# A mixture-of-experts kernel: the order in which an expert's tokens are laid over its 64 slots

## The reference, cut to what matters

```python
def hierarchical_moe(h, wg_router, bg_router, we_router, be_router, w_gate, w_up, w_down):
    g_sel = jnp.argmax(g_logits, axis=-1)
    ...
    top_v, top_i = lax.top_k(e_in, TOP_K_EXPERTS)
    ...
    for g in range(N_GROUPS):
        a = jnp.einsum('nd,edf->nef', hf, w_gate[g])
        b = jnp.einsum('nd,edf->nef', hf, w_up[g])
        hid = jax.nn.silu(a) * b * gates[:, g, :, None].astype(hf.dtype)
        out = out + jnp.einsum('nef,efd->nd', hid, w_down[g])
```

## Time and profile before

| what | value |
|---|---|
| runs of the kernel before | 1487.17, 1493.5, 1494.14 us; median 1493.5 us |
| profiled execution: span, first to last instruction | 1483.8 us |
| profiled execution: its own time | not given beside the span; the fastest run shown is 3.4 us above the span, the median 9.7 us |
| PE busy over the span | 1401.5 us (94%) |
| DVE, ACT, POOL busy | 888.6, 427.9, 57.3 us |
| granted PE clock, mean | 0.989 |
| bytes moved by DMA | 202.00 MB |

### The profile page before, as it was taken

One profiled execution on the slowest core, in us unless ns is written; L12 is line 12 of the kernel. 1 busy time (PEld: TensorE's weight loads), 2 busy tenths in 40 slices (PEclk: granted clock), 3 DMA queues, 4 the chain that ended last, 5 costly groups with the idle time before them and its releaser, 6 DMA issues. The chain is left out here.

```text
span 1483.8 us, 15654 instructions
## 1 busy us (share of the span) xinstructions
PE 1401.5 (94%) x5612; PEld 833.3 (56%) x5612; DVE 888.6 (60%) x1951; ACT 427.9 (29%) x706; POOL 57.3 (4%) x114
## 2 busy tenths in 40 slices
PE   7999999999999989999999999998899798999886
PEld 3455555657567758888887444445485445333222
DVE  5567688898897947767476449965473424222111
ACT  2434444454445315101112233134413430000000
POOL 0000000000000000000000000000000001122211
PEclk9999999999999999999999999999999999999999
DMA  7031010122110124232233121001123658999995
GB/s 293 29 114 57 29 57 29 58 72 65 49 58 29 43 107 164 85 109 90 95 137 109 49 83 60 15 15 78 63 80 127 272 197 322 402 407 405 409 411 174
DMA packets 38972, 202.00 MB, mean 136 GB/s; under 512 B 6896, under 2 KB 8816, under 8 KB 32112
## 3 DMA queue, kind: packets, MB, share of 16 engines
q1 hardware_dynamic: 31600, 186.29, 33.2%
q0 software_dynamic: 4608, 8.40, 2.3%
q10 hardware_dynamic: 2688, 6.29, 1.1%
HBM read 196.77 MB, written 12.58 MB: 141 GB/s over the span
## 5 line engine op out<-in xcount | busy, mean ns | idle before, releaser
L565 PE MATMUL gla_proj<-hT,weight_slots 128*128 128x512 f32 x672 | 295.1, 592 | 1.9 <-DVE hT L1035 1.9
L565 PEld LDWEIGHTS gla_proj<-hT,weight_slots 128*128 128x128 f32 x672 | 125.1, 190 | 147.7 <-issue 146.9
L3328 PE MATMUL moe_banks<-weight_slots,moe_room 128*64 128x512 f32 x400 | 95.2, 626 | 14.9 <-DMA weight_slots<-in_w_gu 12.3
L2062 PE MATMUL mid_p_proj<-hT,weight_slots 128*128 128x512 f32 x208 | 93.0, 594 | 1.8 <-PEq L187 1.8
L3485 DVE SCALAR_TENSOR_TENSOR moe_room<-moe_banks,moe_kept,moe_room 128x256 f32<-128x256 f32 x16 | 7.7, 484 | 131.1 <-ACT moe_room L3440 131.1
L734 ACT ACTIVATE gla_level_decay<-gla_level_decay 128x1024 f32<-128x1024 f32 x56 | 59.1, 1055 | 49.5 <-DVE gla_level_decay L922 49.1
L3328 PEld LDWEIGHTS moe_banks<-weight_slots,moe_room 128*64 128x64 f32 x400 | 29.7, 143 | 71.8 <-issue 56.4
L2062 PEld LDWEIGHTS mid_p_proj<-hT,weight_slots 128*128 128x128 f32 x208 | 39.1, 190 | 52.1 <-issue 52.1
L692 ACT COPY gla_raw<-gla_proj 128x512 f32<-128x512 f32 x38 | 22.4, 589 | 137.5 <-PE gla_proj L565 137.5
L593 PEld LDWEIGHTS gla_level<-gla_level_q,gla_level_k 128*128 128x128 f32 x448 | 55.0, 192 | 8.4 <-issue 6.7
L593 PE MATMUL gla_level<-gla_level_q,gla_level_k 128*128 128x128 f32 x448 | 56.4, 275 | 0.9 <-DVE gla_level_k L933 0.9
(11 more groups left out here) (529 smaller groups left out, 2658.4 us busy)
## 6 DMA issues: line engine op xcount, KB each, us to landing
weight_slots<-in_w_gu SPq DMA_DIRECT2D x25, 2048.0 KB, 22.7
weight_slots<-in_w_gla SPq DMA_DIRECT2D x40, 512.0 KB, 3.6
weight_slots<-in_w_dn SPq DMA_DIRECT2D x10, 2048.0 KB, 28.8
weight_slots<-in_w_merge SPq DMA_DIRECT2D x32, 512.0 KB, 4.8
weight_slots<-in_w_out SPq DMA_DIRECT2D x16, 512.0 KB, 4.4
weight_slots<-in_w_v SPq DMA_DIRECT2D x3, 2048.0 KB, 7.4
hT<-in_w_gu SPq DMA_DIRECT2D x3, 2048.0 KB, 36.6
weight_slots<-in_w_u SPq DMA_DIRECT2D x8, 512.0 KB, 4.4
```

What stands on the lines that cost most here:

```text
L565: last = nc.tensor.matmul(pj[:, n % 2, :], lhsT, rhs, start=(k == 0), stop=(k == KT - 1))
L2062: last = nc.tensor.matmul(pw[:, n % 2, :], a, b, start=(k == 0), stop=(k == KT - 1))
L3328: last = nc.tensor.matmul(pG[rows, e, :], hgT[:, k, rows], core.as_gate_up(at[k // 4])[:, x, k % 4, :], start=(k == 0), stop=(k == KT - 1))
```

## The change

A new constant `slot_rank` holds, for each of the 64 slots, the rank of the token that sits in it. It is loaded into 64 new columns of `moe_kept` (`rank_of`). Both comparisons that make `at_slot` use it in place of 0 to 63. The first 64 ranks go, in order, to the slots

```diff
-        kept = ctx.enter_context(nc.sbuf_tensor("moe_kept", [P, 2 * NB + CAP + 8 * NB + NB + 2 * (P + 4) + 4 + 8], F32))
+        kept = ctx.enter_context(nc.sbuf_tensor("moe_kept", [P, 2 * NB + 2 * CAP + 8 * NB + NB + 2 * (P + 4) + 4 + 8], F32))
...
+        self.rank_of = take(CAP)
...
         sp.dma_start(iota, dram["moe_iota"][:, 0:CAP]).then_inc(aux, 16)
+        sp.dma_start(lot.rank_of, dram["slot_rank"][:]).then_inc(aux, 16)
         core.load_part(sp, 6)
...
-        pe.wait_ge(aux, 80)
+        pe.wait_ge(aux, 96)
...
-        dve.wait_ge(aux, 80)
+        dve.wait_ge(aux, 96)
...
-        chain(equal(at_slot, CAP, slot))
+        chain(nc.vector.tensor_tensor(at_slot, lot.rank_of.unsqueeze(1).to_broadcast([P, 2 * NB, CAP]),
+                                      slot.unsqueeze(2).to_broadcast([P, 2 * NB, CAP]), ALU.is_equal))
...
+    rank = np.arange(CAP)
+    turn, pick = (rank // 8) % 2, rank % 8
+    place = 8 * pick + 4 * ((pick // 4) ^ turn) + rank // 16
+    slot_rank = np.zeros(CAP, np.float32)
+    slot_rank[place] = rank
+    extra["slot_rank"] = np.ascontiguousarray(np.broadcast_to(slot_rank, (P, CAP)))
```

More of the change, by code:

```diff
@@ L3530, in list_rounds @@
                 chain(equal(at_unit[:, :, (n - 1) * EXPERTS:n * EXPERTS], EXPERTS, lot.unit_off))
-            chain(equal(at_slot, CAP, lot.slot))
+            chain(nc.vector.tensor_tensor(at_slot, lot.rank_of.unsqueeze(1).to_broadcast([P, 2 * NB, CAP]),
+                                          lot.slot.unsqueeze(2).to_broadcast([P, 2 * NB, CAP]), ALU.is_equal))
             nc.vector.tensor_tensor(slot_id, at_slot, lot.ids.unsqueeze(2).to_broadcast([P, 2 * NB, CAP]), ALU.mult)
```

## The result

Six runs of the changed kernel give a median of 1480.22 us (1477.86 to 1481.35), six of the one before 1490.93 us (1486.85 to 1494.14; three of them are those shown ahead of the prediction, with the higher median of 1493.5). The ratio is 0.9935, 95% interval 0.9919 to 0.9951: 9.7 us faster at 1490.93 us (7.3 to 12.1), against 8.0 forecast. The whole time lies 5.3 us under the 1485.5 us forecast: 2.6 us because I took 1493.5 for the kernel before, 2.7 because the medians are 10.7 us apart and not 8.0.

A forecast was written before the change was run, and what follows sets the result against it. DMA engines were taken to bound the expert loop, the fullest setting its end. Gains of 6.6 + 1.1 + 0.3 = 8.0 us, taken from the 1493.5 us median, gave 1485.5 us, range 1478 to 1491.

The forecast's parts named there:

- What bounds it: Expert loop: DMA engines bound it; they drop out one after another after 1440 us, the fullest setting the end.
- Rule B: Rows to engines by 8 * (partition >> 6) + ((partition >> 2) & 7): fullest engine goes from 93 rows to 71.
- A: Row-to-engine rule giving the fullest engine 64 rows over the mean, up to 34 us; the prediction excluded it.
- Rule C: Row-to-engine rule making the new order the uneven one, 128 rows against 78: slower, 1520 us, chance 0.02.
- Part 45 lands sooner: Load for the second half of pair 15's gate and up: lands at 1453.7 instead of 1460.27, gain 6.6 us.
- the factor 0.75: Loop's end: the fullest engine's measured excess over the counted one, 10.4 to 13.9 us, used to scale row costs.
- 16.1 us of unchanged work: From pair 15's second gate and up half (1460.27) to the last scatter (1476.39): no slack, stays the same.
- The last scatter: End of the kernel: fullest engine goes from 8 rows to 5, gain 1.1 us, bound 1.5.
- The first gather: Start of the loop, PE waits its 4.1 us in full: fullest engine from 8 rows to 6, gain 0.3 us.
- the perfectly even case: Rival for the loop's end: the 7 rows left over weigh nothing, gain 10.9 us, 1482.6 us, chance 0.12.
- Late issue: Rival: engines drop out because the last parts were issued late; only 1.4 us gained, 1492.1 us, chance 0.17.
- Slow engines: Rival: the last engine is slow by nature, not full; engines 7 and 15 get more rows, 1507 us, chance 0.04.

The follow-up runs named there:

- uneven by B: The change with another rank table, 121 rows on the fullest engine and 8 on the emptiest by Rule B: 1501.64 us, ratio to before 1.0089.
- mirrored: The change's table replaced by the old order read backwards (rank 0 in slot 63), engines 7 and 15 fullest: 1488.26 us, ratio to before 1.0001.
- even by B: The change with another rank table, 75 rows on the fullest engine and 50 on the emptiest by Rule B: 1479.13 us, ratio to before 0.9936.
- rotated: The change with each eight ranks starting three engines further on, 69 rows on the fullest engine instead of 71: 1476.76 us, ratio to before 0.9912.

## Why the prediction was right, point by point

- **What bounds it.** Right. The area under the shares gave an even finish at 1462.4, 224.0 us after the first gather. The changed kernel's area from 1440 to 1470 is 5 x 5.22 = 26.1 us, at 1.01 gone by 1465.8, 223.5 us after its first gather. The mean engine has the same work to the same time; only the last one moved.
- **Rule B.** Right. Two tables that split A from B, 22 us apart in their medians, and six that lie within 2 us of one line of B's counts show it. Rule C falls with the change itself, which is as uneven by C as can be (128 and 0) and got faster. The Trainium skill's formula (DMA: Bandwidth & Descriptors, the section on the descriptor swizzle) names the engines for a transfer of 128 partitions; what the runs add is that it holds, as far as counts can show, for an indirect DMA with part of its rows skipped: a skipped row leaves its engine nearly free and moves nobody else's. Nearly, since it still counts as a packet: with every row skipped, POOL's queue had 3744 packets in 1260 to 1430 and took 1.2% of the 16 engines' time, some 9 ns a packet.
- **Part 45 lands sooner (6.6 us, and 0.3 through the first gather).** Right in kind, 1.4 us too small. PE's last half started 8.3 us sooner after the first gather. The term that was mis-sized is the 7 rows left over, for which I took 2.7 us by the factor 0.75. The PE row at 1467.29 waits for part 47 until then, 225.0 us after the first gather; taken with the even finish of 224.0 or 223.5 that leaves 1.0 to 1.5 us. The spacing behind it was right: 11.5 us from the wait for part 45 to that for part 47, 11.4 forecast.
- **16.1 us of unchanged work.** Nearly. In the old timeline the down matmuls of pair 14 started at 1467.78 after 0.77 us marked as issue; in the changed one they follow at once, and the stretch takes 15.3 us in every even order. I had taken all of it for work, but these 0.8 us were a wait for weights, for part 46. Its load was issued at 1410.50 before and at 1406.60 with the change, and the DMA rows of these issues (the last number is us from issue to landing) are, before and changed:

```profile
weight_slots<-in_w_dn SPq DMA_DIRECT2D x1, 2048.0 KB, 57.2
```

```profile
weight_slots<-in_w_dn SPq DMA_DIRECT2D x1, 2048.0 KB, 55.4
```

So part 46 landed at 1467.7 before, just as the matmuls started, and at 1462.0 with the change, half a us before they did.
- **The last scatter (1.1 us).** From its issue to the end of the span 7.4 us before, 6.7 and 7.0 with the change, 7.5 with the order uneven by B and 7.9 mirrored. From issue to landing it took 5.8 us before, 5.8 uneven by B and 6.3 mirrored, against 5.1 and 5.4 with the change, 4.9 even by B and 5.3 rotated: the two groups don't overlap, and their means are 0.8 us apart. The sign is right and the size about two thirds; "under 5 us" came true in one of the four even profiles only.
- **The first gather (0.3 us).** 4.14 us before, 3.98 and 3.93 now, 3.86 and 3.90 in the other even orders. The gather gained 0.2 us, but PE's turn behind it took 1.98 us instead of 1.53, in the uneven orders too, so nothing of it was left behind the turn.
- **The comparison and the new load.** Nothing, as forecast: the 128x512 comparison takes 0.70 us in the chain as before, and the load stands at 1190.55 to 1190.98, before anything waits. From the stage's first load to the first gather it is 56.5 us in both profiles.

Of the rivals, the perfectly even case was closer to the 9.9 us than the forecast was: its 10.9 us (10.7 with the 1.1 us that the forecast has for the last scatter; its own sum says 1.3) is 1.0 too much, the 8.0 are 1.9 too little. The rows that were left over weighed little, 1.0 to 1.5 us, so the truth lies between the two. From 8.0 to 9.9 the parts add up as 1.4 more through part 45, 0.8 more through part 46 and about 0.4 less in the last scatter. Late issue fell twice: SP's last issues of the changed kernel (start, us) take as long, to 1435.8 here and to 1440.8 before, yet the steps are gone,

```profile
1411.70 24.07 SPq L256 DMA_DIRECT2D weight_slots<-in_w_dn  x2
```

and all engines are busy for 19 us behind it; and without rows there are no steps with the same order of loads. Slow engines fell with the mirror, and the Trainium skill's note that engines 7 and 15 are usually slower (the same page, the section on latency and other measured facts) doesn't show here: with 93 and 84 rows on them the whole time is the one that engines 0 and 8 gave, within 0.14%.

**What stays open.** Why a gather's unevenness is worth next to nothing when the scatters are gone. On the mean engine gathers do cost: by the DMA rows of 1260 to 1430 SP's loads (packets, MB, share of 16 engines) move 71.76 MB without any rows,

```profile
q1 hardware_dynamic: 4924, 71.76, 99.4%
```

and 68.70 MB with the gathers alone:

```profile
q1 hardware_dynamic: 4715, 68.70, 94.8%
```

So the gathers take their part of the bandwidth. PE's pace isn't what hid the gain: with gathers alone its last half of gate and up still waited for part 45, until 1438.64 in the old order and 1437.84 in the new. How gathers share an engine with the loads when they are the only rows was not followed up.

## What to carry to other kernels

Here a stream of large loads kept all DMA engines busy, a transfer with part of its rows skipped still loaded the engines by partition, and the last loads ended with the fullest of them. Where that is so, count the rows for each engine over the whole stream, not for one transfer, and deal them evenly; here each row off the fullest engine was worth 0.45 us, and the order of slots was free to choose. The falling share at the end of such a stream is the measure: its area gives the even finish, and the distance from there to the last landing (10.4 us before, 1.0 to 1.5 after) is what dealing can bring to the stream.

## What the runs showed that I had not expected

- A scatter row with an add costs about twice a gather row. POOL's queue in 1260 to 1430 (packets, MB, share of 16 engines) with scatters only, with gathers only, and with every row skipped, all in the old order:

```profile
q0 software_dynamic: 3600, 3.21, 10.3%
```

```profile
q0 software_dynamic: 3744, 3.41, 5.9%
```

```profile
q0 software_dynamic: 3744, 0.02, 1.2%
```

Less the 1.2%, and over the rows that the MB make at 4 KB each, that is 0.32 us for a scatter row and 0.15 us for a gather row.
- The end doesn't move by a row's price alone. Taking the scatters away brought 26.5 us in the old order, 0.41 us a row over 16 engines, but 16.9 us in the change's order (235.5 to 218.6), 0.26 us a row. The rest of the 26.5 was the unevenness that went with them.
- Without any rows PE is busy 138.7 of 140 us from 1260 to 1400, so there it takes part in the bound.
- The first 1240 us, which are the same in all these kernels, scatter by nearly 4 us between executions (first gather at 1238.45 to 1242.33). A change of 0.6% in the last fifth is read better from a point at its start than from the whole time.
